# Sixteen gate tiles of a two-block kernel moved out of the merge stage and into earlier stages, in plain fp32

## What is computed

```python
p = _split_in(x @ w_in[l])                # q, k, v ... of four mixers A, B, C, D, and "gate"
ya = _mixer_a(...)                        # dilated attention
yb = _mixer_b(...)                        # attention over keys chosen by an index score, lax.top_k(score, 128)
yc = _mixer_c(...)                        # gated linear attention in chunks
yd = _mixer_d(...)                        # delta rule with decays
ys = jnp.stack([ya, yb, yc, yd], axis=2)
gates = jax.nn.sigmoid(p["gate"].reshape(bsz, seq, N_BRANCHES, D_MODEL))
merged = jnp.sum(gates * jnp.einsum('bsnc,ncd->bsnd', ys, w_branch[l]), axis=2)
x = _layer_norm(DN_ALPHA * x + merged @ w_out[l], ln_g[l, 0], ln_b[l, 0])
```

## Time and profile before

| | us |
|---|---|
| three runs | 3665.24, 3668.62, 3679.70 (median 3668.62) |
| profiled execution, its time | 3665.9 |
| profiled execution, its span | 3664.1 |
| PE busy | 3048.2 (83%) |
| DVE busy | 1734.7 (47%) |
| POOL busy | 1522.0 (42%) |
| first block up to `merge` | 0 to 695 |
| `merge` | 695 to 927 |

### The profile page before, as it was taken

The page is one execution under the profiler, slowest core; times in us unless marked ns, Lnnn a source line. Parts: engine busy times, 40 slices in busy tenths (PEclk is TensorE's granted clock), DMA queues, the critical chain, the costliest instruction groups (busy, mean ns, idle before and its releaser), DMA issues. The chain is left out here.

```text
span 3664.1 us, 33431 instructions
## 1 busy us (share of the span) xinstructions
PE 3048.2 (83%) x12858; PEld 2257.0 (62%) x12858; DVE 1734.7 (47%) x2065; ACT 646.1 (18%) x1005; POOL 1522.0 (42%) x430
## 2 busy tenths in 40 slices
PE   6939448899879999394689989999785689989998
PEld 5715237588556666273258867878562368768877
DVE  2174455444266666413464427860214554438840
ACT  0012210100135554303130010000102220010000
POOL 5600000277311111262017756767451037657776
PEclk9955569799979999696699999999896799989999
DMA  3300000122248887221202222222221212212223
GB/s 136 134 14 31 1 0 1 47 92 92 94 183 324 329 317 270 88 91 51 28 12 92 95 78 80 92 92 92 78 80 39 28 42 97 92 58 92 97 87 115
DMA packets 77126, 353.82 MB, mean 97 GB/s; under 512 B 30908, under 2 KB 31292, under 8 KB 38374
## 3 DMA queue, kind: packets, MB, share of 16 engines
q1 hardware_dynamic: 62824, 333.03, 25.4%
q10 hardware_dynamic: 2902, 10.13, 0.9%
q0 software_dynamic: 11232, 8.43, 0.8%
HBM read 357.39 MB, written 30.83 MB: 106 GB/s over the span
## 5 line engine op out<-in xcount | busy, mean ns | idle before, releaser
L129 POOL TENSOR_TENSOR w_hi<-w_raw,w_zero 128x2048 fp32r<-128x2048 f32 x174 | 627.6, 3607 | 1697.9 <-PE bank L156 1645.3
L156 PE MATMUL bank<-xh,w_hi 128*128 128x512 f32 x1864 | 750.1, 402 | 93.5 <-DVE xl L404 50.1
L132 POOL TENSOR_TENSOR w_lo<-w_raw,w_hi 128x2048 fp32r<-128x2048 f32 x174 | 813.2, 4674 | 13.7
L157 PE MATMUL bank<-xl,w_hi 128*128 128x512 f32 x1864 | 745.8, 400 | 0.0
L158 PE MATMUL bank<-xh,w_lo 128*128 128x512 f32 x1864 | 745.2, 400 | 0.0
L156 PEld LDWEIGHTS bank<-xh,w_hi 128*128 128x128 f32 x1864 | 355.3, 191 | 199.4 <-issue 44.0
L158 PEld LDWEIGHTS bank<-xh,w_lo 128*128 128x128 f32 x1864 | 355.3, 191 | 87.6
L157 PEld LDWEIGHTS bank<-xl,w_hi 128*128 128x128 f32 x1864 | 356.1, 191 | 84.8
L499 DVE TENSOR_TENSOR part<-sig,bank 128x512 f32<-128x512 f32 x96 | 66.1, 688 | 381.7 <-PE bank L158 381.3
L2121 DVE TENSOR_TENSOR fl<-work,fh 128x512 fp32r<-128x512 f32 x44 | 211.2, 4800 | 1.5
L536 DVE SCALAR_TENSOR_TENSOR res<-res,bank 128x512 f32<-128x512 f32 x40 | 27.5, 688 | 377.1 <-PE bank L158 377.1
(11 more groups left out here) (497 smaller groups left out, 4800.4 us busy)
## 6 DMA issues: line engine op xcount, KB each, us to landing
w_raw<-weights SPq DMA_DIRECT2D x216, 1024.0 KB, 4.8
raw<-weights SPq DMA_DIRECT2D x51, 1024.0 KB, 6.3
res<-weights SPq DMA_DIRECT2D x26, 1024.0 KB, 6.1
distance_bias<-distance_bias_once ACTq DMA_DIRECT2D x8, 512.0 KB
na_bias<-grid_bias SPq DMA_DIRECT2D x16, 240.0 KB, 7.0
strips<-distance_bias SPq DMA_DIRECT2D x8, 448.0 KB, 3.2
raw<-picked_rows SPq DMA_DIRECT2D x6, 512.0 KB, 5.9
tabs<-tables SPq DMA_DIRECT2D x2, 1408.0 KB, 6.4
```

The costliest lines, as they stand in the source:

```text
L129: pool.tensor_tensor(self.hi[:, s, :], self.raw[:, s, :], self.zero[:, 0:1].to_broadcast([128, CHUNK]), ALU.add).then_inc(self.rounded, 1)
L132: pool.tensor_tensor(self.lo[:, s, :], self.raw[:, s, :], self.hi[:, s, :].bitcast(F32), ALU.subtract).then_inc(self.split, 1)
L156: self.released(pe.matmul(out, hi, moving[0], start=start, stop=False))
L157: pe.matmul(out, hi, moving[1], start=False, stop=False)
```

## The change

Gate tiles 0, 2, 4, ..., 30 (`EARLY`) are no longer made in `merge`. A new class `EarlyGates` makes them earlier, eight plain fp32 matmuls each, with unsplit weights straight from the two `w_raw` slots and an unsplit copy of x (`whole_x`, 2 MB, loaded at the start of `select_keys`). PE writes them to banks 6 and 7 by turns, ACT copies each to `gate_rows`, SP stores it to HBM. The numbers of tiles: six in `select_keys`, two in C's first stage, one in C's `head_norm`, two, two and three in D's first three stages. In `merge` ACT loads them back four ahead and takes the sigmoid in place. The room for `whole_x` comes from `w_hi` and `w_lo`, which now exist only in `project` and from `merge` on; so `project` no longer splits a chunk ahead, `delta_chunks` loads two raw chunks, and `merge` begins by splitting one.

```diff
+PROJECT_CHUNKS = 13
+LATE_GATES = (1, 3, 5, 7)
+EARLY = [u for u in range(4 * KT) if u % 8 not in LATE_GATES]
+EARLY_CHUNKS = len(EARLY) // 2
...
+class EarlyGates:
...
+    def begin(self, sp):
+        sp.dma_start(self.x[:, :, :], self.k.dram["xT"]).then_inc(self.x_in, 16)
+        for chunk in range(2):
+            self.load(sp, chunk)
+
+    def fill(self, pe, n):
+        if self.blocks == 0:
+            pe.wait_ge(self.x_in, 16)
+        for b in range(self.blocks, self.blocks + n):
+            j, t = divmod(b, KT)
+            c = b // 16
+            if b % 16 == 0:
+                pe.wait_ge(self.loaded[c % 2], 16 * (c // 2 + 1))
+            if t == 0 and self.banks[j] in self.banks[:j]:
+                before = max(i for i in range(j) if self.banks[i] == self.banks[j])
+                pe.wait_ge(self.copied, before + 1)
+            mm = pe.matmul(self.k.bank[self.banks[j]][:, :], self.k.ws.raw[:, c % 2, 128 * (b % 16):128 * (b % 16) + 128],
+                           self.x[:, t, :], start=t == 0, stop=t == KT - 1)
...
+    def copy(self, act, n):
+        for j in range(self.n_copied, self.n_copied + n):
+            act.wait_ge(self.made, j + 1)
+            if j >= 2:
+                act.wait_ge(self.stored[j % 2], 16 * (j // 2))
+            act.activation(self.rows[:, j % 2, :], self.k.bank[self.banks[j]][:, :], ACT.Copy).then_inc(self.copied, 1)
...
+    def move(self, sp, n):
+        for j in range(self.n_stored, self.n_stored + n):
+            sp.wait_ge(self.copied, j + 1)
+            sp.dma_start(self.out[j, :, :], self.rows[:, j % 2, :]).then_inc(self.stored[j % 2], 16)
+            if j % 2 and j // 2 + 2 < self.tiles // 2:
+                self.load(sp, j // 2 + 2)
...
+    def end(self, sp):
+        assert self.n_stored == self.tiles
+        for s in self.stored:
+            sp.wait_ge(s, 8 * self.tiles)
...
@@ merge, tensor
+                        if u not in early:
+                            for t in range(KT):
+                                last = ws.product(pe, g[:, :], (k.xh[:, t, :], k.xl[:, t, :]), t == 0, t == KT - 1)
+                            last.then_inc(gate_ready, 1)
@@ merge, scalar
+                    if u in early:
+                        e = early_before(u)
+                        act.wait_ge(ahead_in[e % 4], 16 * (e // 4 + 1))
+                        act.activation(ahead[:, e % 4, :], ahead[:, e % 4, :], ACT.Sigmoid).then_inc(sigmoid_ready, 1)
+                        if e >= 1 and e + 3 < len(early):
+                            act.wait_ge(banks_free, early[e - 1] + 1)
+                            ahead_load(e + 3)
+                        continue
...
@@ select_keys: behind the scores, the relus, and on SP
+            k.gates.fill(pe, 48)
+            k.gates.begin(sp)
+            k.gates.move(sp, 6)
+            k.gates.copy(act, 6)
...
@@ mixer_d, third stage: at the end of each engine's list
+                k.gates.fill(pe, 24)
+                k.gates.move(sp, 3)
+                k.gates.end(sp)
                     act.wait_ge(exps_used, p + 1)
+                k.gates.copy(act, 3)
...
+                k.ws.blocks, k.ws.skipped = 16 * PROJECT_CHUNKS, EARLY_CHUNKS
...
+                    k.gates.clear(nc)
```

More of the change, by code:

```diff
@@ L167, in product_tm, with halves_of_weights, __init__, load @@
         return last
+@contextmanager
+def halves_of_weights(k):
+    with memory(k, w_hi=("r", SLOTS, CHUNK), w_lo=("r", SLOTS, CHUNK)) as (k.ws.hi, k.ws.lo):
+        yield
+class EarlyGates:
+    def __init__(self, k, nc, ctx, first_chunk, tiles, banks, out):
+        self.k, self.first, self.tiles, self.banks, self.out = k, first_chunk, tiles, banks, out
+        self.loaded = [ctx.enter_context(nc.semaphore(f"gate_w_loaded{s}")) for s in range(2)]
+        self.x_in = ctx.enter_context(nc.semaphore("gate_x_in"))
+        self.made = ctx.enter_context(nc.semaphore("gate_made"))
+        self.copied = ctx.enter_context(nc.semaphore("gate_copied"))
+        self.stored = [ctx.enter_context(nc.semaphore(f"gate_stored{s}")) for s in range(2)]
+        self.blocks = self.n_copied = self.n_stored = 0
+    def load(self, sp, chunk):
+        sp.dma_start(self.k.ws.raw[:, chunk % 2, :], self.k.ws.dram[self.first + chunk, :, :]).then_inc(
+            self.loaded[chunk % 2], 16)
+    def begin(self, sp):
[15 more added lines that the diff above has]
+                           self.x[:, t, :], start=t == 0, stop=t == KT - 1)
+            if t == KT - 1:
+                mm.then_inc(self.made, 1)
+        self.blocks += n
+    def copy(self, act, n):
[4 more added lines that the diff above has]
+            act.activation(self.rows[:, j % 2, :], self.k.bank[self.banks[j]][:, :], ACT.Copy).then_inc(self.copied, 1)
+        self.n_copied += n
+    def move(self, sp, n):
[4 more added lines that the diff above has]
+                self.load(sp, j // 2 + 2)
+        self.n_stored += n
+    def end(self, sp):
+        assert self.n_stored == self.tiles
+        for s in self.stored:
+            sp.wait_ge(s, 8 * self.tiles)
+    def clear(self, nc):
+        assert self.n_copied == self.tiles and self.blocks == KT * self.tiles
+        for s in (self.x_in, self.made, self.copied, *self.loaded, *self.stored):
+            nc.sync.sem_clear(s)
+        nc.all_engine_barrier()
@@ L1002, in mixer_c @@
     head_norm(k, [dict(src=k.yb[:, 4 + p, :], scale=1.0 / 64, eps=k.eps[:, 1:2], finish=finish(p))
-                  for p in range(2)])
+                  for p in range(2)], k.gates)
 def mixer_d(k, pj, av, cv):
@@ L1027, in mixer_d, with _ @@
         with stage(k, "vector_order") as (block, order):
+            @block.tensor
+            def _(pe):
+                k.gates.fill(pe, 16)
+            @block.scalar
+            def _(act):
+                k.gates.copy(act, 2)
+            @block.sync
+            def _(sp):
+                k.gates.move(sp, 2)
             @block.vector
@@ L2187, in tm_blocks, with first_gates @@
     return w.reshape(k // 128, 128, f // 128, 128).transpose(0, 2, 1, 3).reshape(-1, 128, 128)
+def first_gates(gate, branch):
+    merged = merge_blocks(gate, branch).reshape(32, 10, 128, 128)
+    late = [merged[u, 8 if u in EARLY else 0:].reshape(-1, 128, 128) for u in range(32)]
+    return merged[EARLY, 0:8].reshape(-1, 128, 128), np.concatenate(late)
 def merge_blocks(gate, branch):
```

97 lines of the change are left out of this document (69 added, 28 removed).

## The result

The kernel before took 3668.1 us (median of 4 runs, 3665.2 to 3679.7), the changed one 3575.4 (4 runs, 3571.7 to 3588.6): a ratio of 0.9748, 95% interval 0.9714 to 0.9782. In a later set of runs the changed kernel gave 3574.2 us (5 runs), 0.9745 [0.9728, 0.9761]. One execution of the last kernel under Experiments (7673.1 us) is more than twice as long as any other and is left out throughout.

A forecast was written before the change was run, and what follows sets the result against it. TensorE was taken to bound `merge`, VectorE the key selection. Terms of 28.9 (C, D), -65.6 (merge) and -1.3 (project) sum to -38.0, from a profiled 3665.9 us to 3628; range 3606 to 3654.

The forecast's parts named there:

- Key selection, six tiles, 0: In the key selection, six early tiles fit while TensorE would idle beside VectorE, with 6.4 us margin: cost 0.
- C and D, +28.9: In the stages of C and D, early tiles outlast each stage's own chain: 28.9 us added together.
- first stage of C: In C's first stage, two early tiles end after the stage's own work: 4.5 us added.
- Third stage: In D's third stage, the third tile waits for ScalarE's copy to free bank 7: +11.4 us (9 to 16).
- the +1 of `clear`: After the early tiles in C and D, one more round of clears and a barrier: +1 us.
- Merge, -65.6: In `merge`, 16 gate tiles fewer but a later start and waits: 166.4 us against 232.0, so -65.6.
- The group changes: In `merge`, TensorE waits 2.5 us for VectorE's multiply at three group changes: 8 us (0 to 20).
- The tail: At the end of `merge`, work left after the products: 4.9 us.
- Project, -1.3: At the end of `project`, GpSimd no longer splits the chunk ahead, so the stage ends 1.3 us earlier.
- The estimate of 7.5 us per tile: Early gate tiles in plain fp32, by the skill page's four passes: 0.933 us per matmul; the forecast used 6.93 per tile.
- the price of a split matmul: In `merge`, 0.2333 us per split matmul, from 7.00 us per unit of 30; 5.60 us per gate tile.
- Rival (a), 3612: C, D and `merge`: clocks stay up (-8), shorter merge tail and free group changes (-8): 3612 us; chance 0.12.

The follow-up runs named there:

- the last kernel under Experiments: Changed kernel with last early tile in bank 4, odd gate tiles early, GpSimd's second chunk waiting for VectorE's split of y: median 3573.0 us, 0.9728.
- The kernel that undoes the alignment alone: Changed kernel with 32 unused bytes per partition on both sides of the split weights: 3628.1 us, 0.9890.
- the second execution: The changed kernel itself profiled once more, nothing altered: span 3572.4 us, 14.4 below its first; timed 3574.2 us.
- the probe: Stand-alone matmul groups at full clock with varied operand start addresses, not the kernel's work: 8 plain fp32 matmuls took 6.86 to 6.87 us.
- the square of four medians: Before 3669.2 us; before plus a 224-byte pad 3618.7; changed with 32-byte pads around the split weights 3628.1; changed 3575.4.
- the left column: The two unaligned kernels: before, 3669.2 us, and changed with 32 unused bytes on both sides of the split weights, 3628.1 us.
- the two probes: Stand-alone groups of 24 split matmuls, varying operand distance, then higher address bits, single operands and width: 5.44 us at distance 0, 5.60 at 32 bytes.
- two kernels: Kernel before with unused 32-byte buffers on both sides of the split weights, 3645.0 us, or only behind them, 3640.7 us.

## Why the prediction was wrong

**Its sum was right for what it counted.** The kernel that undoes the alignment alone took 3628.1 us; the sum said 3628. That the two agree to 0.1 us is luck: the forecast took 38.0 us off a profiled execution of 3665.9, and the measurement is 41 us below a median of 3669.2, with an interval of 32 to 49. In its trace the first block gains 42.3 us (933.36 for 975.68), and what follows takes 5.1 us longer than before (2684.3 for 2679.2), of which the experts' matmuls explain 2. In the same trace the merge, with the old spacing, starts at 718.05 and ends with the last of these:

```profile
718.05 0.43 DVE L589 CAST yh<-yb 128x512 fp32r<-128x512 f32 x1 [1.74 <-PEq L246]
...
883.36 0.69 DVE L604 TENSOR_TENSOR ml<-part,mh 128x512 fp32r<-128x512 f32 x1
```

That is 166.0 us, for the 166.4 of the prediction. The trace of after against the terms, after minus before:

- *Key selection, six tiles, 0*: held. The 96 records of the fill took 43.8 us, for 41.6 + 2.5, DVE's stretch is as long as before, and the attention begins some 5 us earlier, by as much as `project` ends.
- *C and D, +28.9*: from the first stage of C to the merge's start the shift went from -5.7 to +22.1, so +27.8 (+23.6 in the second execution, where the clock was up earlier). Piece by piece: first stage of C 1.9 + 5.7 = +7.6 for 4.5 (the fill took 16.4 us in this trace, 14.0 in the other), `head_norm` and shift stage 8.2 - 1.9 = +6.3 for 7, second stage +5.0 for 5. Third stage: +10.4 for 11.4, and what follows -1.5 for the +1 of `clear`. So the first piece was 3 us too low and the end 3.5 too high, and the total is closer than its parts. The wait came as forecast: PE idle for 12.33 us, for some 10, until ACT's copy.
- *Merge, -65.6*: 232.0 to 161.9, -70.1, of which 576 x 6.67 ns = 3.8 are the spacing, so -66.3. PE started at 733.41, 16.2 us after the stage's first instruction, for 16. The group changes cost 7.8 us in three waits of up to 2.6, for 8 and 2.5. The tail was 2.7 us (876.3 to 879.05), for 4.9.
- *Project, -1.3*: -4.9 by the first ACT instruction of the next stage (181.75 and 176.80), of which the spacing makes 21 groups x 0.16 = 3.4. In the kernel that undoes the alignment the next stage began 2.7 us earlier than before (179.06 against 181.75).

By the page of the Trainium skill "SBUF — State Buffer" (section SBUF: two separate sides) the loser of the port pair that DVE and GpSimd share waits for the other's whole instruction. The traces agree again: 3.97 and 4.78 us for DVE's instructions beside POOL's 3.81 and 4.88. "FP8 and Floating Point Precision" of the Trainium skill (section TensorE Precision Notes) gives true fp32 four passes. The estimate of 7.5 us per tile made from it was too high: the probe took 6.87 us for 8 plain fp32 matmuls at full clock, beside 5.44 to 5.60 for 24 split ones. The passes themselves no trace shows.

**The step that failed** is the first one, the price of a split matmul: "one unit of 30 matmuls, so 0.2333 us per matmul", taken as fixed. It was a property of where two buffers stood in before, and the change moved them. I had read the change as work that moves, and left out that `halves_of_weights` and the scoped buffers change the address of every operand. So the sum has no term for it, in the merge or in the stages that the change leaves alone. The term that was missing is 7416 x 6.67 ns = 49 us (measured 53) over the whole program, more than the sum of all the others. None of my rivals had it: each was about waits and clocks within the stages that change. Rival (a), 3612, was on the right side for other reasons. Its free group changes didn't come (they cost 7.8 us); for its 8 us from clocks, C and D came out 1 us below my forecast in one trace and 5 in the other; its shorter tail came, by 2 us. The range was built from the terms' bounds, and a term that is not there has none.

That the alignment and not the early tiles causes the spacing is shown by the square of four medians and by the groups in the four traces (5.60 in the left column, 5.44 in the right); that it is the distance modulo 256 bytes, by the two probes, but for the open case at 64 bytes. What inside the chip makes a matmul wait is not shown.

## What to carry to other kernels

When a change adds, drops or moves an SBUF buffer, compare the start addresses of stationary and moving operands of the hot matmuls before and after, and time an unused pad of 32 to 224 bytes as an experiment of its own: here one pad of 224 bytes in the kernel before was worth about as much as the restructuring. A spacing that stays the same from group to group, as the 5.60 us did here, can still be a property of the program and not of the chip; if it moves in stages that a change doesn't touch, look for something global first. And when a wait at a stage's start is shortened, look for what its end sets free: here PE's earlier start let POOL's next chunk in, which held the engine that PE needed next.

## What the runs showed of the hardware

- fp32r matmuls of 128x128 by 512 columns in the order `xh` by `w_hi`, `xl` by `w_hi`, `xh` by `w_lo` follow each other every 0.2267 us where all operands stand alike modulo 256 bytes, about every 0.229 us at a distance of 64 bytes (0.2333 in one stage of two kernels), and every 0.2333 us at other multiples of 32 up to 224, all at a granted clock of 1.00. At 384 columns, of the distances 0, 32 and 64 bytes, only 32 cost (0.08 us for 24), at 256 columns none. Plain fp32 (0.858 us per 512 columns in the probe) took the same at each distance tried.
- One operand of four that stands 32 bytes off costs 0.12 to 0.16 us per 24 matmuls of the 0.16 that all off cost.
- The same fill of 32 records took 16.4 us in one execution and 14.0 in another: in the first the granted clock was 0.50 for its first 4 us, in the second 1.00 from its start.
- Beside GpSimd instructions of 3.81 and 4.88 us, VectorE instructions between SBUF buffers that take 0.69 and 0.42 us alone took 3.97 and 4.78.
